# A fused decoder kernel: values of the sparse heads with the values stationary, and the weights divided by their sum on GpSimd

## The chip, the cores and the metric

The kernel runs on one core of a Trainium2 chip. The metric is the device time of one execution in microseconds (us). The core's engines each run a program of their own and wait for one another by semaphores: TensorE (PE, matmuls and transposes), VectorE (DVE), ScalarE (ACT), GpSimd (POOL), and the DMA queues. The kernel before takes 2286.29 us, the median of three runs (2286.06 to 2287.71).

## What is computed

A first block (attention, mLSTM, mixture of experts) feeds a second block of two equal layers over 512 tokens of width 1024. Each layer of the second has two kinds of attention, 8 sparse heads of 64 columns and 4 dense ones, then gates and an FFN. The change is in the sparse heads of the second block:

```
def sparse_attention(q, k, v, q_idx, k_idx, w_idx, k_sel):
    ...
        logits = jnp.einsum('bqhd,bqkhd->bqhk', qb, kg) * (dh ** -0.5)
        logits = jnp.where(valid[:, :, None, :], logits, -jnp.inf)
        p = jax.nn.softmax(logits, axis=-1).astype(v.dtype)
        return jnp.einsum('bqhk,bqkhd->bqhd', p, vg)
    ...
    ya = sparse_attention(aq, ak, av, iq, ik, iw, k_sel).reshape(B, S, D_A)
    ...
    g = jax.nn.sigmoid((gates + gate_bias))
    g_a, g_b = jnp.split(g, 2, axis=-1)
    merged = g_a * (ya @ w_up_a) + g_b * (yb @ w_up_b)
    x = x + merged @ w_out
```

The selection of the best 128 keys is done with a mask over all earlier keys, so the products run over whole rows of keys.

## The kernel before

**Units.** The attention stage of a layer (`pe_att2`) runs 48 units, one for each head of a block of 128 tokens: 0 to 15 are the dense heads (blocks 0 to 3), 16 to 47 the sparse heads, eight for each of blocks 4 to 7, which are the token rows i = 0 to 3 with 128(i+1) keys. A unit passes through the engines in steps. In step s TensorE makes the scores of units s and s+1 (sparse heads in pairs, on the row halves of the array, L1469), transposes the weights of unit s-3 (L1479, "turn") and multiplies those of unit s-4 with the values (L1487: one matmul for each 128 keys and head, stationary 128 turned weights, moving the 64 columns of the values). VectorE finds the least value of each row (L1493), ScalarE the exponential with its sum (L3426); the turned weights are copied out of PSUM by ScalarE for even units (L1504) and by VectorE for odd ones (L1502). After the last head of a sparse block VectorE takes the reciprocal of the eight sums (L3380) and multiplies the block's output by it (L3383); TensorE turns the block with four transposes (L1512, `pe_block_turned`); ScalarE and VectorE split it into a rounded high part and the rest (L1519, L1526).

**Dense work between.** Between these come parts of the big matmuls (`pe_between`), three to a step up to s = 31, then two, then one from s = 49. Each part is three kinds of matmuls (L686 to L688: high by high, low by high, high by low). The parts are counted by y. Parts 0 to 47 are the projections of the sparse heads; 48 to 111 use the gate's weight pieces 0 to 15, four parts to a piece; 112 to 119 are the places of the block turns, with no matmuls of weights; 120 to 135 use pieces 16 to 19, of the first up projection.

**Weight pieces.** Each piece comes by DMA, ScalarE makes its rounded high half (L637), GpSimd (in this stage) the low half, weights less high half (L674, `pool_lo`), and waits for nothing but the high half. The high halves have three buffers: that of piece p is made when the products of piece p-3 are done. Each engine's program is in fixed order. On GpSimd the stage is only the twenty low halves of a layer, in a row; ScalarE has its high halves between exponentials, copies and splits.

The profiled kernel's functions that the change touches:

## Time and profile before

| what | value |
|---|---|
| median of three runs | 2286.29 us |
| span of the profiled execution (its own time) | 2288.9 us |
| TensorE busy | 2188.9 us (96%) |
| VectorE, ScalarE, GpSimd busy | 54%, 37%, 16% |
| attention stage of the second block, first layer | about 842 to 1066 us |
| the same in the second layer | the same rows 788.4 us later |

A row of the timeline gives the start of a group of instructions, its length, and in brackets the idle time of the engine before it with what ended it. Consecutive instructions of a kind stand in one row with their count. Matmuls overlap in the rows: what one costs is the distance from its start to the next start. A row of a line's group gives how many, their busy time and the mean of one in ns. TensorE's granted clock is 1.00 at 2.4 GHz and 0.50 at 1.2 GHz.

### The profile page before, as it was taken

What the parts mean: (1) busy time and instruction counts of PE and PEld (TensorE: products, weight loads), DVE (VectorE), ACT (ScalarE), POOL (GpSimd) and SP (SyncE); (2) the same over time, 40 slices, a digit from 0 to 9 for tenths busy, and PEclk for the clock granted to TensorE, in tenths of its full rate; (3) what the DMA queues carried; (4) which work ended last, traced back from release to release, by engine and by line L of the source; (5) the groups of instructions that cost most, each with busy time, mean ns of one, the idle gap of its engine ahead of it and who ended that gap; (6) DMA issues with size and microseconds to landing.
All of it is one profiled execution on the core that took longest, in us unless ns stands there. A gap on an engine that the chain in (4) does not pass through costs nothing.

```text
span 2288.9 us, 28099 instructions
## 1 busy us (share of the span) xinstructions
PE 2188.9 (96%) x10757; PEld 1671.8 (73%) x10757; DVE 1238.6 (54%) x2370; ACT 847.1 (37%) x1493; POOL 358.4 (16%) x276
## 2 busy tenths in 40 slices
PE   7999998799998999999999999999999999999999
PEld 4786776543436767778788888877677787888887
DVE  4744557621326876675544334469667755453442
ACT  4444544311105455443432222344654433231231
POOL 0111124010002544320000000045433200000000
PEclk9999999889999999999999999999999999999999
DMA  8217301699992222212233232232222122323222
GB/s 303 66 47 230 129 29 48 251 385 409 409 407 87 74 74 56 82 57 65 84 110 101 94 99 92 81 91 83 66 64 82 51 81 92 102 92 101 92 86 80
DMA packets 175580, 288.01 MB, mean 126 GB/s; under 512 B 13486, under 2 KB 125656, under 8 KB 175448
## 3 DMA queue, kind: packets, MB, share of 16 engines
q1 hardware_dynamic: 173152, 278.73, 36.2%
q0 software_dynamic: 1152, 4.19, 0.5%
q10 hardware_dynamic: 1144, 3.29, 0.4%
q8 instruction: 87, 1.43, 0.2%
q14 instruction: 45, 0.37, 0.1%
HBM read 281.98 MB, written 4.19 MB: 125 GB/s over the span
## 4 chain that ended last, share of the span: by engine, by line
PE 80%; DVE 10%; DMA 3%; ACT 3%; issue 2%; SPq 1%; POOL 0%; DVEq 0%; ACTq 0%
PE PS L686 21%; PE PS L688 20%; PE PS L687 20%; PE PS L2496 4%; PE PS L1487 3%; PE PS L2537 2%; PE PS L1469 2%; PE PS L2557 1%; PE PS L1479 1%; SPq L3701 1%; DMA AR<-in_w_mod_dram 1%; DVE AL L868 1%; PE PS L1121 1%; PE PS L1667 1%; DVE CO L865 1%
## 5 line engine op out<-in xcount | busy, mean ns | idle before, releaser
L686 PE MATMUL PS<-OPH,WHI 128*128 128x512 f32 x1192 | 482.0, 404 | 5.5 <-DVE AR L1318 2.8
L688 PE MATMUL PS<-OPH,WLO 128*128 128x512 f32 x1192 | 467.7, 392 | 0.0
L687 PE MATMUL PS<-OPL,WHI 128*128 128x512 f32 x1192 | 466.5, 391 | 0.0
L637 ACT ACTIVATE WHI<-RAW 128x1024 fp32r<-128x1024 f32 (+2 forms) x282 | 292.9, 1041 | 457.4 <-PE PS L688 449.5
L658 DVE TENSOR_TENSOR WLO<-RAW,WHI 128x1024 fp32r<-128x1024 f32 (+1 forms) x187 | 224.3, 1202 | 368.7 <-ACT WHI L637 368.3
L674 POOL TENSOR_TENSOR WLO<-RAW,WHI 128x1024 fp32r<-128x1024 f32 (+1 forms) x95 | 229.8, 2422 | 928.9 <-ACT WHI L637 922.8
L686 PEld LDWEIGHTS PS<-OPH,WHI 128*128 128x128 f32 x1192 | 225.2, 189 | 61.0 <-issue 10.1
L688 PEld LDWEIGHTS PS<-OPH,WLO 128*128 128x128 f32 x1192 | 224.8, 189 | 48.5
L687 PEld LDWEIGHTS PS<-OPL,WHI 128*128 128x128 f32 x1192 | 225.5, 189 | 42.2 <-issue 1.0
L686 PE MATMUL PS<-WHI,OPH 128*128 128x512 f32 (+2 forms) x568 | 226.6, 399 | 9.0 <-DVE OPL L2196 2.5
L688 PE MATMUL PS<-WHI,OPL 128*128 128x512 f32 (+2 forms) x568 | 216.0, 380 | 0.0
L687 PE MATMUL PS<-WLO,OPH 128*128 128x512 f32 (+2 forms) x568 | 215.2, 379 | 0.0
L686 PEld LDWEIGHTS PS<-WHI,OPH 128*128 128x128 f32 x568 | 108.2, 190 | 46.4 <-issue 23.9
L686 PE MATMUL PS<-FR,WHI 128*128 128x512 f32 x352 | 136.9, 389 | 0.0
L687 PE MATMUL PS<-FR,WHI 128*128 128x512 f32 x352 | 136.9, 389 | 0.0
L688 PE MATMUL PS<-FR,WLO 128*128 128x512 f32 x352 | 136.9, 389 | 0.0
L688 PEld LDWEIGHTS PS<-WHI,OPL 128*128 128x128 f32 x568 | 108.1, 190 | 19.8
L687 PEld LDWEIGHTS PS<-WLO,OPH 128*128 128x128 f32 x568 | 108.3, 191 | 15.5 <-issue 0.5
L3426 ACT ACTIVATE AL<-AL,AC 128x128 f32<-128x128 f32 (+3 forms) x128 | 71.2, 557 | 106.2 <-DVE AC L1493 105.7
L686 PEld LDWEIGHTS PS<-FR,WHI 128*128 128x128 f32 x352 | 66.1, 188 | 13.8
L688 PEld LDWEIGHTS PS<-FR,WLO 128*128 128x128 f32 x352 | 66.1, 188 | 13.7
L687 PEld LDWEIGHTS PS<-FR,WHI 128*128 128x128 f32 x352 | 66.1, 188 | 13.6
(469 smaller groups left out, 3314.6 us busy)
## 6 DMA issues: line engine op xcount, KB each, us to landing
RAW<-in_w_in_dram SPq DMA_DIRECT2D x102, 512.0 KB, 3.7
RAW<-in_w_ffn_in_dram SPq DMA_DIRECT2D x88, 512.0 KB, 3.5
RAW<-in_w_ffn_out_dram SPq DMA_DIRECT2D x40, 512.0 KB, 3.4
RAW<-in_w_mod_dram SPq DMA_DIRECT2D x36, 512.0 KB, 4.7
ONCE<-in_w_down_dram SPq DMA_DIRECT2D x35, 512.0 KB, 15.8
RX<-in_w_gate_dram SPq DMA_DIRECT2D x29, 512.0 KB, 15.4
RAW<-in_w_out_dram SPq DMA_DIRECT2D x24, 512.0 KB, 3.4
RAW<-in_w_up_dram SPq DMA_DIRECT2D x20, 512.0 KB, 15.7
```

The source lines that it names most:

```text
L637: hi.up(A.e.activation(q.fhi, q.flat, ACT.Copy), ("w", q.i))
L658: lo_v.up(V.e.tensor_tensor(q.flo, q.flat, q.fhi.bitcast(F32), ALU.subtract), ("w", q.i))
L674: lo_p.up(G.e.tensor_tensor(q.flo, q.flat, q.fhi.bitcast(F32), ALU.subtract), ("w", q.i))
L686: T.e.matmul(o, a[0], b[0], start=first, stop=False)
L687: T.e.matmul(o, a[0], b[1], start=False, stop=False)
L688: return T.e.matmul(o, a[1], b[0], start=False, stop=last)
L865: t = row_v.up(V.e.tensor_reduce(c[:, 0:k], s3[:, n0:, :], X, ALU.add), (r, "sum"))
L1469: mm = T.e.matmul(PS[:, 512 * b + c0:512 * b + c0 + w], l_, r_, start=True, stop=True)
L1487: mm = T.e.matmul(u.o, u.pt[:, 128 * j:128 * j + 128], v_, start=(j == 0), stop=(j == nb - 1))
L2496: mm = T.e.matmul(PS[64 * i:64 * i + 64, 512 * b:512 * b + 512], XG[:, g % 3, 2 * n + k, 64 * i:64 * i + 64], q.raw[:, k, :], start=(n == ...
L2537: mm = T.e.matmul(PS[64 * i:64 * i + 64, o:o + 512], AE[:, g % 2, k, 64 * i:64 * i + 64], q.raw[:, 0, 512 * n:512 * n + 512], start=(k == ...
L3426: expd.up(A.e.activation(v.p, v.p, ACT.Exp, bias=v.nm, scale=-1.0, accum_out=v.rs), v.name)
```

## The change

The values of a sparse head become the stationary operand (64 columns) and the 128 turned weights move. Two heads of a pair use the two column halves of the array, so the output of a block comes out with the head's columns on partitions and tokens along the row: it is turned already. The values of both heads of a pair are issued together, at the odd head's step (`pe_pair_values`). The block turns of blocks 4 to 7 are gone, 16 transposes for each layer; the splits read PSUM itself (blocks 6 and 7) or a copy that VectorE makes of it (blocks 4 and 5). As a row's sum now lies along the moving side, the weights are divided ahead of their turn: VectorE takes the reciprocals of a pair's sums at each even step, and GpSimd multiplies each unit's weights by them (`evened`, new line L3007). TensorE's turn of a unit waits for that in place of the exponential. The low halves of the weight pieces are placed between the units on GpSimd by a rule of due parts. The copies of turned weights get four buffers in place of two. Line numbers grow by one up to the stage, by more in it (L674 is L675, L637 is L638, L1479 is L1480, L3426 is L3465).

```diff
pool_rope(rope_no[("aq", l), 0] + 4 * at[0] + at[1])
-            for pieces in J["gate", l] + J["upb", l]:
-                for i in pieces:
-                    pool_lo(i + 3)
+            units = units2(l)
+            later_ = [i + 3 for pieces in J["gate", l] + J["upb", l] for i in pieces]
+            y = 48
+            for s in range(16, len(units) + 2):
+                while later_ and y >= GATES0 + 4 * (20 - len(later_)) + 6:
+                    pool_lo(later_.pop(0))
+                if s >= 18:
+                    u = units[s - 2]
+                    G.wait_ge(*tidy["over", l, u.no])
+                    evened.up(G.e.tensor_scalar(u.p, u.p, u.over, None, ALU.mult), u.name)
+                y += parts_at(s)
+            for upto in later_:
+                pool_lo(upto)
...
                         pe_block_turned_b(l, i)
-                if y in (TURN0 + 5, TURN0 + 6):
-                    blk = y - TURN0 - 1
-                    pe_block_turned(("a2", l, blk), YR2[:, blk % 4], tidy["a2", l, blk], D)
...
                 if y in (TURN0 + 6, TURN0 + 7):
-                    blk = y - TURN0 - 2
-                    act_block_split(("a2", l, blk), OPH[:, 0:4, sparse_tokens(blk)])
+                    act_value_split(l, y - TURN0 - 2)
...
                 if y in (TURN0 + 6, TURN0 + 7):
-                    blk = y - TURN0 - 2
-                    c = sparse_tokens(blk)
-                    dve_block_split(("a2", l, blk), OPL[:, 0:4, c], OPH[:, 0:4, c])
+                    dve_value_split(l, y - TURN0 - 2)
...
         PTB2 = in_(AL, 23456, 1024).rearrange("p (i n) -> p i n", i=2)
-        YR2 = in_(AL, 14752, 2048).rearrange("p (i n) -> p i n", i=4)
+        PTC2 = in_(AL, 14752, 1024).rearrange("p (i n) -> p i n", i=2)
+        YT2 = in_(AL, 15776, 1024).rearrange("p (i g n) -> p i g n", i=2, g=4)
...
                     u.vs = [VAR[:, j, 64 * h:64 * h + 64] for j in range(i + 1)]
-                    u.o = ps(OUT2)[:, 64 * h:64 * h + 64]
+                    u.o = PS[hp:hp + 64, 512 * OUT2 + 128 * pr:512 * OUT2 + 128 * pr + 128]
+                    u.over = a8[:, 32 + h:33 + h]
...
-                u.pt = PTB2[:, u.no % 2, 0:u.n]
+                ring = PTB2 if u.kind == "b" or u.no % 4 < 2 else PTC2
+                u.pt = ring[:, u.no % 2, 0:u.n]
...
+        def turned_free(l, u):
+            if u.no in (18, 19):
+                return row_v[rope_no[("ak", l), 3], "done"]
+            return weighed["u", l, u.no - (2 if u.no < 18 else 4)]
...
-            return tidy["a2", l, blk], tidy["a2", l, blk]
+            done = tidy["a2", l, blk] if blk < 6 else split_v["a2", l, blk]
+            return done, done
+        def pe_pair_values(l, pair_):
+            for u in pair_:
+                T.wait_ge(*copied["pt", u.full])
+            n = len(pair_[0].vs)
+            for j in range(n):
+                for u in pair_:
+                    mm = T.e.matmul(u.o, u.vs[j], u.pt[:, 128 * j:128 * j + 128], start=(j == 0), stop=(j == n - 1))
+            weighed.up(mm, *[u.full for u in pair_])
+        def value_of(blk):
+            return YT2[:, blk - 4] if blk < 6 else ps(OUT2).rearrange("p (g n) -> p g n", g=4)
+        def act_value_split(l, blk):
+            if blk < 6:
+                A.wait_ge(*tidy["a2", l, blk])
+                A.wait_ge(*prod["gate", l, 7, 1])
+            else:
+                A.wait_ge(*weighed["u", l, 8 * blk - 9])
+            split_a.up(A.e.activation(OPH[:, 0:4, sparse_tokens(blk)], value_of(blk), ACT.Copy), ("a2", l, blk))
+        def dve_value_split(l, blk):
+            c = sparse_tokens(blk)
+            V.wait_ge(*split_a["a2", l, blk])
+            split_v.up(V.e.tensor_tensor(OPL[:, 0:4, c], value_of(blk), OPH[:, 0:4, c].bitcast(F32), ALU.subtract),
+                       ("a2", l, blk))
...
                     u = units[s - 3]
-                    T.wait_ge(*(diff_v["mix", l, u.no] if u.kind == "b" else expd[u.name]))
+                    T.wait_ge(*(diff_v["mix", l, u.no] if u.kind == "b" else evened[u.name]))
...
                         T.wait_ge(*copied[(u.kind + "v", l), t])
-                    pe_values(u, u.full)
-                    if u.blk == 7 and u.h == 3:
-                        pe_block_turned(("a2", l, 6), YR2[:, 2], tidy["a2", l, 6], D)
+                    if u.kind == "b":
+                        pe_values(u, u.full)
+                    elif u.h % 2:
+                        pe_pair_values(l, units[s - 5:s - 3])
                 some(dense, parts_at(s) - 2)
-            some(dense, 1)
-            pe_block_turned(("a2", l, 7), YR2[:, 3], tidy["a2", l, 7], D)
...
-            B.give(OUT2, (tidy, ("a2", l, 7)))
+            B.give(OUT2, (split_v, ("a2", l, 7)))
...
             for s in range(len(units) + 5):
+                if 18 <= s < len(units) + 2 and s % 2 == 0:
+                    u = units[s - 1]
+                    a8 = AC8[:, u.blk % 2, :]
+                    V.wait_ge(*expd[u.name])
+                    tidy.up(V.e.reciprocal(a8[:, 31 + u.h:33 + u.h], a8[:, 7 + u.h:9 + u.h]), ("over", l, u.no - 1), ("over", l, u.no))
...
                         if u.no >= 2:
-                            V.wait_ge(*weighed[units[u.no - 2].full])
+                            V.wait_ge(*turned_free(l, u))
...
                                   ("yb", l, u.blk))
-                    if u.last_head and u.kind == "a":
-                        a8 = AC8[:, u.blk % 2, :]
-                        V.wait_ge(*expd[u.name])
-                        t = tidy.up(V.e.reciprocal(a8[:, 32:40], a8[:, 8:16]))
-                        V.wait_ge(*t)
+                    if u.last_head and 4 <= u.blk < 6:
                         V.wait_ge(*weighed[u.full])
-                        tidy.up(V.e.tensor_tensor(YR2[:, u.blk % 4].rearrange("p (h e) -> p h e", h=8),
-                                                  ps(OUT2).rearrange("p (h e) -> p h e", h=8),
-                                                  a8[:, 32:40].unsqueeze(2).to_broadcast([128, 8, 64]), ALU.mult),
-                                ("a2", l, u.blk))
-                    if u.blk == 7 and u.h == 3:
-                        dve_block_split(("a2", l, 6), OPL[:, 0:4, sparse_tokens(6)], OPH[:, 0:4, sparse_tokens(6)])
+                        tidy.up(V.e.tensor_copy(YT2[:, u.blk - 4], ps(OUT2).rearrange("p (g n) -> p g n", g=4)), ("a2", l, u.blk))
+                    if u.last_head and u.blk >= 6:
+                        dve_value_split(l, u.blk)
...
                         if u.no >= 2:
-                            A.wait_ge(*weighed[units[u.no - 2].full])
+                            A.wait_ge(*turned_free(l, u))
...
-                    if u.blk == 7 and u.h == 3:
-                        act_block_split(("a2", l, 6), OPH[:, 0:4, sparse_tokens(6)])
+                    if u.last_head and u.blk >= 6:
+                        act_value_split(l, u.blk)
```

On GpSimd, before, the stage of a layer stands between the rotary steps of one stage and those of the next (WLO<-RAW,WHI are the low halves of weight pieces):

```order
L851 TENSOR_TENSOR AL<-AL 128x8x32 [waits row_v,row_a]
L851 TENSOR_TENSOR AL<-AL 128x8x32
L674 TENSOR_TENSOR WLO<-RAW,WHI 128x1024 [waits hi] x20
L674 TENSOR_TENSOR WLO<-RAW,WHI 128x648 [waits hi] x4
L851 TENSOR_TENSOR AL<-AL,RS 128x4x32 [waits row_v,row_a]
```

The twenty low halves follow one another with nothing between them. On GpSimd now, from the second unit of a pair (unit 37) to unit 45; AL<-AL,AC is a unit's weights times the reciprocals; the three low halves are those of pieces 17, 18 and 19:

```order
L3007 TENSOR_SCALAR AL<-AL,AC 128x384 [waits tidy]
L675 TENSOR_TENSOR WLO<-RAW,WHI 128x1024 [waits hi]
L3007 TENSOR_SCALAR AL<-AL,AC 128x384
L3007 TENSOR_SCALAR AL<-AL,AC 128x512 [waits tidy]
L675 TENSOR_TENSOR WLO<-RAW,WHI 128x1024 [waits hi]
L3007 TENSOR_SCALAR AL<-AL,AC 128x512
L3007 TENSOR_SCALAR AL<-AL,AC 128x512 [waits tidy]
L675 TENSOR_TENSOR WLO<-RAW,WHI 128x1024 [waits hi]
L3007 TENSOR_SCALAR AL<-AL,AC 128x512
L3007 TENSOR_SCALAR AL<-AL,AC 128x512 [waits tidy]
```

Behind low half 18 stand units 41 and 42, behind low half 19 units 43 to 47. On ScalarE, before, from the exponential of unit 43 over the copy of unit 40 and the splits of blocks 4 and 5 to the high halves of pieces 18 and 19 (WHI<-RAW):

```order
L3426 ACTIVATE AL,AC<-AL,AC 128x512 [waits least]
L1504 ACTIVATE AL<-PS 128x512 [waits turned,weighed]
L1519 ACTIVATE OPH<-PS 128x4x128 x2
L637 ACTIVATE WHI<-RAW 128x1024 [waits prod,raw2]
L3426 ACTIVATE AL,AC<-AL,AC 128x512 [waits least] x2
L1504 ACTIVATE AL<-PS 128x512 [waits turned,weighed]
L637 ACTIVATE WHI<-RAW 128x1024 [waits prod,raw3]
```

High half 18 follows two block splits. On ScalarE now, the same stretch:

```order
L3465 ACTIVATE AL,AC<-AL,AC 128x512 [waits least]
L1505 ACTIVATE AL<-PS 128x512 [waits turned,weighed]
L3315 ACTIVATE OPH<-PS 128x4x128 [waits weighed]
L3315 ACTIVATE OPH<-AL 128x4x128 [waits prod]
L3315 ACTIVATE OPH<-AL 128x4x128
L638 ACTIVATE WHI<-RAW 128x1024 [waits raw2]
L3465 ACTIVATE AL,AC<-AL,AC 128x512 [waits least] x2
L1505 ACTIVATE AL<-PS 128x512 [waits turned]
L638 ACTIVATE WHI<-RAW 128x1024 [waits prod,raw3]
```

The split of block 6 (from PSUM) stands ahead of the other two now, and high half 18 one split later. On TensorE, before, from the turn of unit 39 to the scores of units 44 and 45 (L1512 are turns of blocks 4 and 5, L1487 values of units 38 and 39):

```order
L1479 MATMUL PS<-cst,AL_64 128x128 [waits copy_a,expd]
L1479 MATMUL PS<-cst,AL_64 128x128 x2
L1512 MATMUL PS<-cst,AL_64 128x128 [waits split_v]
L1512 MATMUL PS<-cst,AL_64 128x128 x3
L1487 MATMUL PS<-AL_64 128x64 x3
L1512 MATMUL PS<-cst,AL_64 128x128 [waits split_v]
L1512 MATMUL PS<-cst,AL_64 128x128 x3
L1479 MATMUL PS<-cst,AL_64 128x128 [waits least,expd]
L1479 MATMUL PS<-cst,AL_64 128x128 x3
L1487 MATMUL PS<-AL_64 128x64 [waits copy_v]
L1487 MATMUL PS<-AL_64 128x64 x2
L1469 MATMUL PS<-AL_64 128x512 [waits least]
```

Two block turns lie between the turns of units 39 and 40. On TensorE now, the same stretch (L1480 turns, L3302 the pair's values):

```order
L1480 MATMUL PS<-cst,AL_64 128x128 [waits copy_a,evened]
L1480 MATMUL PS<-cst,AL_64 128x128 x2
L1480 MATMUL PS<-cst,AL_64 128x128 [waits least,evened]
L1480 MATMUL PS<-cst,AL_64 128x128 x3
L3302 MATMUL PS<-AL_64 64x128 [waits copy_v]
L3302 MATMUL PS<-AL_64 64x128 x5
L1470 MATMUL PS<-AL_64 128x512 [waits least]
L1470 MATMUL PS<-AL_64 128x512
```

The two block turns are gone, the values of unit 38 have moved behind the turn of unit 40 and joined those of 39, and each turn waits for GpSimd's `evened`.

## Rows read from the trace of the kernel before

**Rows 1.** The page: busy time, share of the span and instructions; shares of the chain.

```profile
PE 2188.9 (96%) x10757; PEld 1671.8 (73%) x10757; DVE 1238.6 (54%) x2370; ACT 847.1 (37%) x1493; POOL 358.4 (16%) x276
...
PE 80%; DVE 10%; DMA 3%; ACT 3%; issue 2%; SPq 1%; POOL 0%; DVEq 0%; ACTq 0%
```

**Rows 2.** Timeline of TensorE, first layer: start us, us, engine, line, operation, idle before.

```profile
1025.90 0.60 PE L1512 MATMUL PS<-cst,AL 128*128 128x128 f32 x4
1026.34 0.78 PE L1487 MATMUL PS<-AL 128*128 128x64 f32 x6
1026.95 0.61 PE L1512 MATMUL PS<-cst,AL 128*128 128x128 f32 x4
...
1031.10 0.60 PE L1479 MATMUL PS<-cst,AL 128*128 128x128 f32 x4
...
1032.93 1.00 PE L1487 MATMUL PS<-AL 128*128 128x64 f32 x8
1033.74 0.47 PE L686 MATMUL PS<-OPH,WHI 128*128 128x512 f32 x1
1034.06 0.39 PE L687 MATMUL PS<-OPL,WHI 128*128 128x512 f32 x1
```

**Rows 3.** Timeline of TensorE: column halves in the MoE; row halves (scores).

```profile
485.95 0.59 PE L2496 MATMUL PS<-FM 128*64 128x512 f32 x1
...
486.38 0.59 PE L2496 MATMUL PS<-FM 128*64 128x512 f32 x1
...
914.69 0.49 PE L1469 MATMUL PS<-AL 64*128 64x128 f32 x4
915.11 0.50 PE L686 MATMUL PS<-OPH,WHI 128*128 128x512 f32 x1
```

**Rows 4.** GpSimd by line and form, whole span: count, busy us, mean ns, idle before.

```profile
L674 POOL TENSOR_TENSOR WLO<-RAW,WHI 128x1024 fp32r<-128x1024 f32 x91 | 223.3, 2456 | 473.2 <-ACT WHI L637 467.1 <-DVE AL L899 6.1
...
L2057 POOL TENSOR_SCALAR AR<-AR,SM 128x128 f32<-128x128 f32 x40 | 24.5, 630 | 31.5 <-PE PS L1934 18.4 <-PE PS L1966 7.6 <-ACT SM L2002 5.5
...
L2060 POOL TENSOR_TENSOR AR<-AR 128x512 f32<-128x512 f32 x1 | 1.3, 1270 | 0.8 <-ACT AR L2024 0.8
...
L670 POOL CAST RH<-cst 128x1024 fp32r<-128x1024 f32 x1 | 1.0, 1042 | 4.4 <-PE PS L1953 4.4
```

**Rows 5.** Timeline of ScalarE, first layer, steps 41 to 46.

```profile
1025.00 0.72 ACT L3145 ACTIVATE AL<-AL,VT 128x512 f32<-128x512 f32 x1 [0.42 <-DVE AL L3196]
...
1028.65 1.08 ACT L1519 ACTIVATE OPH<-PS 128x512 fp32r<-128x512 f32 x2
1029.61 1.08 ACT L637 ACTIVATE WHI<-RAW 128x1024 fp32r<-128x1024 f32 x1
...
1037.30 1.06 ACT L637 ACTIVATE WHI<-RAW 128x1024 fp32r<-128x1024 f32 x1 [0.80 <-PE PS L688]
```

**Rows 6.** Timeline of GpSimd, first layer: low halves of pieces 18 and 19.

```profile
1030.77 2.40 POOL L674 TENSOR_TENSOR WLO<-RAW,WHI 128x1024 fp32r<-128x1024 f32 x1 [17.36 <-ACT WHI L637]
1038.44 2.40 POOL L674 TENSOR_TENSOR WLO<-RAW,WHI 128x1024 fp32r<-128x1024 f32 x1 [5.28 <-ACT WHI L637]
```

**Rows 7.** Timelines of VectorE and of TensorE, first layer, steps 20 and 21.

```profile
930.19 0.29 DVE L1493 CUSTOM_DVE_ANT_0 AL<-PS,AL 128x128 f32<-128x128 f32 x1
...
932.42 0.47 PE L686 MATMUL PS<-OPH,WHI 128*128 128x512 f32 x1
```

**Rows 8.** Timeline of TensorE, first layer: end of piece 16, turn of unit 43.

```profile
1036.81 0.40 PE L688 MATMUL PS<-OPH,WLO 128*128 128x512 f32 x1
...
1040.53 0.60 PE L1479 MATMUL PS<-cst,AL 128*128 128x128 f32 x4
```

**Rows 9.** Stretches: us, busy us of each engine (instructions), granted clock, DMA, GB/s.

```profile
105.70:108.10 2.40, 0.04 (x1) 0.00 (x0) 2.10 (x4) 2.40 (x6) 0.00 (x0) 1.00 0.00 0
108.40:111.80 3.40, 3.40 (x18) 3.40 (x18) 2.02 (x3) 0.44 (x1) 0.00 (x0) 0.50 0.05 8
1020.00:1030.00 10.00, 9.47 (x71) 7.56 (x72) 8.44 (x19) 8.66 (x19) 0.00 (x0) 1.00 0.00 1
```

More of the change, by code:

```diff
@@ L417, in body @@
     least, expd, sank, tidy = signal("least"), signal("expd"), signal("sank"), signal("tidy")
+    evened = signal("evened")
     gate_v, gate_a = signal("gate_v"), signal("gate_a")
@@ L3403, in dve_att2 @@
                 some(index_, best_at(s))
-            dve_block_split(("a2", l, 7), OPL[:, 0:4, sparse_tokens(7)], OPH[:, 0:4, sparse_tokens(7)])
             for _ in dense:
@@ L3449, in act_att2 @@
                 some(dense, parts_at(s))
-            act_block_split(("a2", l, 7), OPH[:, 0:4, sparse_tokens(7)])
             for _ in dense:
```

## The prediction

> **What bounds the kernel now.** I read the page's busy line and chain first: TensorE is busy for 96% of the span and 80% of the chain that ended last is TensorE [rows 1]. Work taken off TensorE is therefore gained wherever no other engine becomes late. The change touches only the attention stage of the second block, once per layer, and the rows of the second layer repeat those of the first 788.4 us later, so I work out one layer and double it. Inside the stage the timelines of TensorE, ScalarE and GpSimd have to be read side by side, since the change gives GpSimd work that TensorE waits for.
>
> **What TensorE is relieved of.** A sparse head's values in block 7 are eight matmuls, now from 1032.93 to 1033.74; the first dense matmul behind them takes 0.32 us to the next instead of 0.23 [rows 2], so a head holds TensorE for about 0.90 us, and a pair of heads 1.79. The eight start 0.11 us apart though only 64 columns move: they are bound by loading the stationary block. Six matmuls of block 6 cost 0.67 in the same way (1026.34 to 1026.95 is 0.61 [rows 2], and 0.06 to 0.09 behind), and by the same pitch the four of block 5 0.445, the two of block 4 0.22. The new form takes 8, 6, 4 or 2 passes per pair, each pass two matmuls on the two column halves. No row shows this form at 128 columns. Its nearest row is the MoE's: two column halves start together and the passes of 512 columns are 0.43 us apart [rows 3], so 128 columns stream in 0.107. I take 0.112 per pass, and 0.33 for going into and out of the halves, an estimate from the row halves of the scores, where two passes of 128 hold TensorE for 0.42 us (914.69 to 915.11 [rows 3]), 0.2 more than they stream, with 0.1 on the first dense matmul behind as there is today. A pair is then 0.55, 0.78, 1.00, 1.22 us in blocks 4 to 7, against 0.45, 0.89, 1.34, 1.79. Over four pairs each: +0.4, -0.5, -1.4, -2.3, together -3.7 us. The bounds of a pass are 0.055 (half of today's load) and 0.21 (the row halves' pass, where load and stream follow each other).
>
> The four block turns, four transposes each, took 0.44 us apiece (1025.90 to 1026.34 [rows 2]): -1.75. Four PSUM splits stay, from another source. So 5.45 us of TensorE work go per layer, 10.9 in both.
>
> **What GpSimd is given.** Before, it made only the low halves of the weight pieces here, 2.40 us each, and idled between. Now it also multiplies the weights of 32 units, in order with the low halves. No row has this instruction at 512 columns. At 128 it took 0.63; two-input work of 512 took 1.27, a one-input cast of 1024 took 1.04 [rows 4]. I take 1.1, between the last two, since one operand here is a scalar per row; bounds 0.8 and 2.5 (0.63 times four).
>
> By the Trainium skill (GPSIMD Engine Reference, Elementwise — side-by-side cycle accounting) a tight loop over 512 elements takes 769 ns, and its section Engine selection prefers VectorE for such work. By that figure each of the two terms below that hold one such instruction would be 0.33 us smaller, 1.3 us less in all. No run here shows it yet.
>
> **Where TensorE waits for it.** The order decides this. In the listing of the changed kernel GpSimd has low half 18 ahead of unit 41 and low half 19 ahead of unit 43. A low half waits for ScalarE's high half of the same piece. In the trace, ScalarE's row is unbroken from 1025.00 (but for issue): exponentials, splits, the copy of unit 40, two block splits, and only then high half 18 at 1029.61 [rows 5]. GpSimd had been idle for 17.4 us then and took low half 18 at 1030.77 [rows 6]. Nobody cared: piece 18 is used much later. Now unit 41 stands behind it.
>
> Shift up to there: values of blocks 4, 5 and half of 6 (+0.4 - 0.5 - 0.7), and one early wait. Unit 18 needs VectorE's reciprocal, which comes no earlier than 930.19; then 0.63 for the unit and 2.46 for low half 4, behind it, give 933.3, with the reciprocal itself some 0.1 more, against TensorE's use of piece 4 at 932.42 [rows 4, 7]: +1.0. Together +0.2. ScalarE has one more split ahead of high half 18 than before (block 6's), 0.54 us. So high half 18 ends at 1029.61 + 0.2 + 0.54 + 1.08 = 1031.4, low half 18 at 1033.9, unit 41 at 1035.0, TensorE's turn of unit 41 at 1035.1. It was at 1031.10 [rows 2]. **At this turn TensorE stands 4.0 us later than before**, whatever it gained ahead of it: the gains of steps 37 to 43 and two block turns are lost in that wait.
>
> Behind it stand four pairs of block 7 (-2.3) and two block turns (-0.9). Then the same again at unit 43: high half 19 waits for the last product of piece 16, whose last matmul starts at 1036.81; ScalarE starts 0.26 after its end (1037.30), 1.06, GpSimd 0.08 and 2.40, unit 43 1.1: 4.9 us after piece 16 [rows 5, 6]. TensorE needs 3.5 from there to the turn at 1040.53 [rows 8], 3.8 with a pair's values in place of a head's: **+1.0**. From unit 44 on GpSimd has only units, one to each step of TensorE, which is longer: nothing waits.
>
> **The clock.** TensorE's granted clock is 1.00 in this stage, between 1020 and 1030 as elsewhere, though no dense matmul runs there [rows 9]. But where it idled 2.4 us (105.70 to 108.10), the next 3.4 us ran at 0.50, 1.2 GHz [rows 9], and other idles of over 2 us in the trace are followed by the like. None of those under 2 us is. The idle ahead of turn 41 is the 4.0 and the gains spent in it, so well over 2. I take such a stretch as likely: half of 3.4, **+1.7**.
>
> **The sum.** Per layer +4.0 - 2.3 - 0.9 + 1.0 + 1.7 = +3.5; both layers +7.0. The profiled execution's span is 2288.9 us, which would become 2296; its runs' median is 2286.3, 2.6 below, so I predict 2286.3 + 7 = **2293 us**, 0.3% slower. What a measurement of this kernel can tell from no change is about 0.2%, 4.6 us. Its own range by the price of unit and pass is 2290 to 2296.
>
> **The rivals.**
> *No fall of the clock.* Same waits, +1.8 per layer: 2290. For it: one idle of over 2 us at the trace's start passed without a fall. Chance 0.21.
> *ScalarE is early enough (ends on the other side).* The place is high half 18. If it ended by 1027.5, low half 18 and unit 41 would be done when TensorE comes, and the 5.45 us less wait 1.0 and some 1.3 in the latency-bound steps 40 to 43 would remain: -3.1 per layer, 2280. It needs ScalarE's row to move up by 4 us; its links are the scores of unit 40 and its own exponentials, which do not get shorter. Against it: the unbroken row. Chance 0.17.
> *Cheap passes.* At 0.055 a pass the shift becomes about -1.8 and block 7's pairs give -4.1 instead of -2.3: some 4 us less per layer, 2285. Chance 0.09.
> *Dear passes.* If load and stream add up (0.107 + 0.055 = 0.16, up to 0.21), block 7 gives -0.6 or +0.8 and the shift ahead of turn 41 grows by 1.9 to 3.5: +3.5 to +6.5 more per layer, 2300 to 2306. Against it: the 128 by 64 loads of the MoE lie wholly beside the stream. Chance 0.10. By the Trainium skill (TensorEngine Tiling (Array Packing), Gotcha 2: Feature Incompatibilities) column tiling excludes the fast weight load, which would make this rival's load long; the MoE's passes at 0.43 for 512 columns show no such cost, though a load could hide there that 128 columns would not.
> *A dear unit.* At 2.4 us per 512 columns both waits grow by 1.3: 2298.5. Chance 0.09.
>
> **How the numbers follow.** Forecast 0.34, no fall 0.21, early ScalarE 0.17, dear passes 0.10, cheap passes 0.09, dear unit 0.09. Slower by over 0.2% (above 2290.9): 0.27 of the forecast, 0.04 of no fall, both dear cases: 0.50. Faster (below 2281.7): early ScalarE, and 0.03 of cheap passes: 0.20. The rest, 0.30, is within. The range 2280 to 2300 leaves out the dear passes and the lower half of early ScalarE, under 2 in 10.
>
> **What would show it.** Right: an idle of TensorE of several microseconds ahead of unit 41's turn (a few before 1035 in the first layer), released by GpSimd's new line, with ScalarE's high half 18 at its root; a smaller one at unit 43; GpSimd's row without gaps from high half 18 to unit 42; granted clock near 0.5 behind turn 41; eight passes of a pair in some 1.2 us. Wrong: turn 41 without an idle, low half 18 starting before 1029, or a pair of block 7 at 1.6 us and more.

## The result, and the profile after

The changed kernel takes 2299.72 us (median of four runs, 2298.13 to 2301.18), the kernel before beside it 2287.0: a ratio of 1.0046, 95% interval 1.0032 to 1.006. Run again beside another set it was 1.0056 (1.0041 to 1.007). Of 2286.3 us that is 7.3 to 16 us; 7 had been forecast. The change makes the kernel slower.

The page of the changed kernel, to be read beside [rows 1] (busy time, share of the span, instructions of each engine):

```profile
PE 2181.3 (95%) x10725; PEld 1649.0 (72%) x10725; DVE 1234.2 (54%) x2390; ACT 846.9 (37%) x1493; POOL 426.8 (19%) x340
```

TensorE is busy for 7.6 us less and GpSimd for 68 us more. So work did leave TensorE; what came is waiting. Whole spans compare badly here, since the first block, which nothing touches, came out between 5.4 us shorter and 1.5 longer from one execution to another, the after shown here 4.0 shorter. The stage itself is compared between the same two matmuls instead: the first with gate piece 0, and one at the stage's end. The timeline of TensorE before, first and second layer (start us, length, engine, line, operation):

```profile
903.54 0.47 PE L686 MATMUL PS<-OPH,WHI 128*128 128x512 f32 x1 [1.31 <-ACT WHI L637]
...
1064.82 0.39 PE L686 MATMUL PS<-OPH,WHI 128*128 128x512 f32 x1
...
1691.94 0.47 PE L686 MATMUL PS<-OPH,WHI 128*128 128x512 f32 x1 [1.31 <-ACT WHI L637]
...
1853.22 0.39 PE L686 MATMUL PS<-OPH,WHI 128*128 128x512 f32 x1
```

The same four matmuls of the changed kernel:

```profile
899.52 0.47 PE L687 MATMUL PS<-OPH,WHI 128*128 128x512 f32 x1 [1.30 <-ACT WHI L638]
...
1066.14 0.39 PE L687 MATMUL PS<-OPH,WHI 128*128 128x512 f32 x1
...
1693.17 0.47 PE L687 MATMUL PS<-OPH,WHI 128*128 128x512 f32 x1 [1.30 <-ACT WHI L638]
...
1860.55 0.39 PE L687 MATMUL PS<-OPH,WHI 128*128 128x512 f32 x1
```

The stage took 161.28 us in both layers; now 166.62 and 167.38: +5.3 and +6.1, together 11.4. In this execution TensorE's work between the layers and behind them moved by under 0.1 us; only the last transfers, of the output, end 0.4 us later. The table gives this difference, to within 0.01 us, for every kernel that follows.

| kernel | layer 1, us | layer 2, us | ratio to the kernel before (95%) |
|---|---|---|---|
| changed | +5.34 | +6.11 | 1.0046 (1.0032 to 1.006) |
| changed, again | +5.34 | +6.24 | 1.0056 (1.0041 to 1.007) |
| weights not divided | -5.46 | -5.40 | 0.9959 (0.9945 to 0.9972) |
| low halves 18, 19 moved | -2.74 | -2.74 | 0.9977 (0.9968 to 0.9986) |
| high half 18 early | -0.94 | -0.95 | 0.9994 (0.9985 to 1.0004) |
| units 41, 43 twice | +11.08 | +10.55 | 1.0106 (1.009 to 1.0121) |
| idle filled | +3.86 | +3.86 | 1.0032 (1.0021 to 1.0043) |
| own reciprocals, low half 4 first | -4.24 | -4.24 | 0.9967 (0.9954 to 0.998) |
| and low halves 16, 17 later | -4.90 | -4.84 | 0.996 (0.9945 to 0.9975) |
| on VectorE, one input | -1.16 | -1.14 | 0.9986 (0.9977 to 0.9995) |
| on VectorE, two inputs | +0.53 | +2.17 | 1.0018 (1.0009 to 1.0027) |

**What TensorE waits for** in the first layer's stage (engine and line, what released it, total us, times, longest):

```profile
PE PS L1480 <- POOL AL L3007: 7.5, 5, 4.5
PE PS L687 <- ACT WHI L638: 1.3, 1, 1.3
PE PS L687 <- issue: 1.1, 1, 1.1
```

The first row is new: five turns wait for GpSimd's multiplication. The second stood before too. Two smaller waits are for VectorE, 0.5 us (there before) and 0.4 us (new). "issue" at L687 is the first use of piece 4, at 929.49; low half 4 had ended on GpSimd just then, at 929.39. The two longest in TensorE's timeline, which answer to [rows 2] and [rows 8]:

```profile
1027.48 0.40 PE L689 MATMUL PS<-OPH,WLO 128*128 128x512 f32 x1
1032.34 1.12 PE L1480 MATMUL PS<-cst,AL 128*128 128x128 f32 x4 [4.47 <-POOL AL L3007]
1033.11 0.78 PE L687 MATMUL PS<-OPH,WHI 128*128 128x512 f32 x1
1033.68 0.63 PE L688 MATMUL PS<-OPL,WHI 128*128 128x512 f32 x1
...
1044.33 0.66 PE L1480 MATMUL PS<-cst,AL 128*128 128x128 f32 x4 [1.54 <-POOL AL L3007]
```

These are the turns of units 41 and 43. Behind the first the matmuls start 0.43 us apart (1033.68, 1034.11, ...) instead of 0.23. GpSimd at the same time, to be read beside [rows 6]:

```profile
1022.14 1.56 POOL L3007 TENSOR_SCALAR AL<-AL,AC 128x512 f32<-128x512 f32 x1 [0.63 <-DVE AC L3385]
1028.39 2.35 POOL L675 TENSOR_TENSOR WLO<-RAW,WHI 128x1024 fp32r<-128x1024 f32 x1 [4.68 <-ACT WHI L638]
1030.72 3.10 POOL L3007 TENSOR_SCALAR AL<-AL,AC 128x512 f32<-128x512 f32 x2
1040.35 2.38 POOL L675 TENSOR_TENSOR WLO<-RAW,WHI 128x1024 fp32r<-128x1024 f32 x1 [6.53 <-ACT WHI L638]
1042.71 7.74 POOL L3007 TENSOR_SCALAR AL<-AL,AC 128x512 f32<-128x512 f32 x5
```

GpSimd finished unit 40 at 1023.7, then idled 4.68 us for high half 18, although unit 41's reciprocal had been there since 1022.04. Low half 18, unit 41, and TensorE goes on at once. ScalarE's row, beside [rows 5]:

```profile
1025.72 0.60 ACT L3315 ACTIVATE OPH<-PS 128x512 fp32r<-128x512 f32 x1
1026.20 1.16 ACT L3315 ACTIVATE OPH<-AL 128x512 fp32r<-128x512 f32 x2
1027.24 1.07 ACT L638 ACTIVATE WHI<-RAW 128x1024 fp32r<-128x1024 f32 x1
...
1039.21 1.06 ACT L638 ACTIVATE WHI<-RAW 128x1024 fp32r<-128x1024 f32 x1 [0.85 <-PE PS L689]
```

Three block splits, then high half 18: the order that the listing had shown. Last the granted clock (stretch, its length, busy us of PE, PEld, DVE, ACT, POOL with counts, then the clock), behind turn 41 in the first layer, behind turn 43 in the first, and behind turn 41 in the second:

```profile
1033.10:1036.50 3.40, 3.40 (x12) 2.75 (x11) 1.23 (x2) 0.00 (x0) 0.73 (x1) 0.62 0.17 57
1044.30:1047.70 3.40, 3.37 (x18) 2.83 (x19) 2.05 (x4) 0.00 (x0) 3.40 (x3) 1.00 0.41 137
1826.00:1829.40 3.40, 3.40 (x11) 2.82 (x12) 0.69 (x1) 0.00 (x0) 1.39 (x1) 0.50 0.36 125
```

Ahead of turn 41 TensorE had idled 4.47 us in both layers, ahead of turn 43 1.54. In the second layer the low clock (1.2 GHz) lasts longer, which is most of the 0.8 us by which that layer is worse.

### The profile page after: what moved, and what is told of

The parts are those of the page before. It is cut to its first block, busy times and chain, and to the rows that moved or that the text cites. A ratio compares the mean times of both kernels' runs of the same rounds, so it can differ in the third digit from the quotient of the medians.

```text
span 2296.6 us, 28115 instructions
## 1 busy us (share of the span) xinstructions
PE 2181.3 (95%) x10725; PEld 1649.0 (72%) x10725; DVE 1234.2 (54%) x2390; ACT 846.9 (37%) x1493; POOL 426.8 (19%) x340
## 4 chain that ended last, share of the span: by engine, by line
PE 77%; DVE 11%; DMA 4%; ACT 4%; issue 2%; POOL 1%; SPq 1%; DVEq 0%; ACTq 0%
PE PS L687 21%; PE PS L689 20%; PE PS L688 20%; PE PS L2497 3%; PE PS L2538 2%; PE PS L1488 2%; PE PS L1470 1%; PE PS L2558 1%; PE PS L1480 1%; SPq L3739 1%; ACT WHI L638 1%; DMA AR<-in_w_mod_dram 1%; DVE AL L869 1%; DVE CO L866 1%; DMA ONCE<-in_w_down_dram 1%
## 5 line engine op out<-in xcount | busy, mean ns | idle before, releaser
L687 PE MATMUL PS<-OPH,WHI 128*128 128x512 f32 x1192 | 480.0, 403 | 7.7 <-DVE AR L1319 2.8
L638 ACT ACTIVATE WHI<-RAW 128x1024 fp32r<-128x1024 f32 (+2 forms) x282 | 293.1, 1041 | 465.0 <-PE PS L689 456.9
L675 POOL TENSOR_TENSOR WLO<-RAW,WHI 128x1024 fp32r<-128x1024 f32 (+1 forms) x95 | 229.6, 2420 | 759.4 <-ACT WHI L638 753.4
L687 PEld LDWEIGHTS PS<-OPH,WHI 128*128 128x128 f32 x1192 | 225.1, 189 | 67.5 <-issue 17.5
L687 PE MATMUL PS<-WHI,OPH 128*128 128x512 f32 (+2 forms) x568 | 226.9, 400 | 9.0 <-DVE OPL L2197 2.5
L687 PEld LDWEIGHTS PS<-WHI,OPH 128*128 128x128 f32 x568 | 108.2, 190 | 46.4 <-issue 24.0
L687 PE MATMUL PS<-FR,WHI 128*128 128x512 f32 x352 | 136.9, 389 | 0.0
L3465 ACT ACTIVATE AL<-AL,AC 128x128 f32<-128x128 f32 (+3 forms) x128 | 71.0, 556 | 111.7 <-DVE AC L1494 111.3
L3007 POOL TENSOR_SCALAR AL<-AL,AC 128x128 f32<-128x128 f32 (+3 forms) x64 | 70.1, 1104 | 119.9 <-DVE AC L3385 119.9
L687 PEld LDWEIGHTS PS<-FR,WHI 128*128 128x128 f32 x352 | 66.1, 188 | 13.7
```

The costliest lines, as they stand in the source:

```text
L638: hi.up(A.e.activation(q.fhi, q.flat, ACT.Copy), ("w", q.i))
L675: lo_p.up(G.e.tensor_tensor(q.flo, q.flat, q.fhi.bitcast(F32), ALU.subtract), ("w", q.i))
L687: T.e.matmul(o, a[0], b[0], start=first, stop=False)
L3007: evened.up(G.e.tensor_scalar(u.p, u.p, u.over, None, ALU.mult), u.name)
L3465: expd.up(A.e.activation(v.p, v.p, ACT.Exp, bias=v.nm, scale=-1.0, accum_out=v.rs), v.name)
```

## Experiments

**The theory** is the prediction's: TensorE's gain is real, and GpSimd's order gives more than all of it back. The rivals: the new form of the values brings nothing; GpSimd is too slow wherever the work stands; the low clock has another cause.

### The values alone

This kernel leaves out the division by the sum: GpSimd has low halves alone, and a turn waits for the exponential again.

```diff
-                if s >= 18:
-                    u = units[s - 2]
-                    G.wait_ge(*tidy["over", l, u.no])
-                    evened.up(G.e.tensor_scalar(u.p, u.p, u.over, None, ALU.mult), u.name)
...
-                    T.wait_ge(*(diff_v["mix", l, u.no] if u.kind == "b" else evened[u.name]))
+                    T.wait_ge(*(diff_v["mix", l, u.no] if u.kind == "b" else expd[u.name]))
```

> The weights are not divided by their sum at all (GpSimd's multiplications are left out, the turns wait for the exponential again); the values in column halves, the splits and the missing block turns stay, so this shows TensorE's side alone. Theory: 5.45 us of TensorE work less per layer, of which some 1.3 is eaten in the steps without dense work: -4 per layer, 2279 us, and no idle of TensorE at a turn. Rival (the new form of the values is itself no gain): 2284 or more.

Measured: ratio 0.9959, -5.46 and -5.40 us in the stage. So the expected -4 per layer was too cautious: the stage loses all of the 5.45 us worked out from the rows, although TensorE has three new waits for VectorE there, 0.8 us together. (The time, 2279.7, is near the expected 2279, but the kernel before took 2288.3 beside it.) A pair of block 7, with the dense matmuls around it (timeline of the changed kernel):

```profile
1049.17 0.40 PE L689 MATMUL PS<-OPH,WLO 128*128 128x512 f32 x1
1049.50 1.09 PE L3302 MATMUL PS<-AL 128*64 128x128 f32 x16
1050.53 0.50 PE L687 MATMUL PS<-OPH,WHI 128*128 128x512 f32 x1
1050.87 0.40 PE L688 MATMUL PS<-OPL,WHI 128*128 128x512 f32 x1
```

0.33 us into it instead of 0.23, 1.03 for it, 0.34 out of it instead of 0.23: 1.24 us, against 1.22 forecast and 1.79 before. Cheap and dear passes both fall.

### GpSimd's order

Low half 18 behind unit 43, low half 19 behind unit 45:

```diff
-                while later_ and y >= GATES0 + 4 * (20 - len(later_)) + 6:
+                while later_ and (y >= GATES0 + 4 * (20 - len(later_)) + 6 if len(later_) > 4 else s >= 54 - 2 * len(later_)):
```

> The changed kernel, with low half 18 on GpSimd moved behind unit 43 and low half 19 behind unit 45; nothing else differs. Theory (the order on GpSimd: unit 41 stands behind a low half that waits for ScalarE): TensorE's idles of 4.5 us at the turn of unit 41 and 1.5 at unit 43 are gone in both layers, with them the stretch at half clock; TensorE comes to turn 41 some 0.6 us later than before by its own work, then gains 3.2, so about -2.5 us per layer against the kernel before, 2282 us. Rival (GpSimd is too slow for both kinds of work wherever they stand): waits of like size come back at units 42 to 47 or at the first use of pieces 18 and 19, 2292 or more.

Measured: ratio 0.9977, -2.74 us in both layers, 8 to 9 us per layer better than the changed kernel. TensorE's waits for GpSimd in this stage:

```profile
PE PS L1480 <- POOL AL L3007: 1.4, 3, 0.7
```

Of 7.5 us 1.4 are left, at units 34, 36 and 40, and no wait came at the pieces 18 and 19. The same work on the same engine, two instructions moved in a row: GpSimd was not too slow.

### ScalarE's order

The other end of the same wait. GpSimd's order stays; ScalarE makes high half 18 at step 40:

```diff
+            elif y == TURN0:
+                act_hi(J["upb", l][0][0] + 3)
```

> The changed kernel with GpSimd's order as it is, but ScalarE makes high half 18 four steps earlier (at step 40, where it idles 3.6 us). Theory: the root of the idle at unit 41 is ScalarE's row, so low half 18 runs behind unit 40 at about 1023.7 to 1026 and the idle at 41 falls from 4.5 us to under 0.5, the half clock with it; the idle at 43 stays near 1.5, since high half 19 waits for piece 16. About -1 us per layer against the kernel before, 2285 us. Rival (GpSimd's own pace): the low half and the unit, 3.9 us together, still leave an idle of 2 us or more at unit 41, 2294.

Measured: ratio 0.9994 (no difference from before), -0.94 us in the stage, as expected. The idle at unit 41 is gone: its turn starts 0.23 us behind the matmul ahead of it, at 1031.09. That at unit 43 is 1.54 as it was. GpSimd here:

```profile
1025.53 1.56 POOL L3007 TENSOR_SCALAR AL<-AL,AC 128x512 f32<-128x512 f32 x1 [0.67 <-DVE AC L3387]
1027.06 2.38 POOL L675 TENSOR_TENSOR WLO<-RAW,WHI 128x1024 fp32r<-128x1024 f32 x1
1029.40 1.57 POOL L3007 TENSOR_SCALAR AL<-AL,AC 128x512 f32<-128x512 f32 x1
```

Low half 18 runs in the gap between units 40 and 41. So the root of the idle at 41 was ScalarE's row, through GpSimd's.

### The price of a unit on that path

```diff
+                    if u.no in (41, 43):
+                        G.wait_ge(*evened.up(G.e.tensor_scalar(u.p, u.p, u.over, None, ALU.mult)))
```

> The changed kernel with units 41 and 43 multiplied a second time on GpSimd (one more instruction of 1.55 us each, ahead of the one that TensorE waits for). Theory: GpSimd's row from high half 18 to turn 41 and from high half 19 to turn 43 is the path, so the idles become 6.0 and 3.1 us, +3.1 per layer at least, 2304 to 2307 us. Rival (TensorE is held there by something else, GpSimd only finishes about then): the time stays within 1 us of the changed kernel's 2298 to 2301.

Measured: ratio 1.0106, +11.08 and +10.55 us in the stage, 5.7 and 4.4 more than the changed kernel. The two turns in TensorE's timeline:

```profile
1039.44 1.11 PE L1480 MATMUL PS<-cst,AL 128*128 128x128 f32 x4 [6.12 <-POOL AL L3009]
...
1054.06 0.66 PE L1480 MATMUL PS<-cst,AL 128*128 128x128 f32 x4 [3.20 <-POOL AL L3009]
```

The idles grew by 1.65 and 1.66, as expected: this row is the path. But the time grew by more than these 3.3 us. The clock in the stretches behind both turns:

```profile
1039.40:1042.80 3.40, 3.36 (x10) 2.88 (x11) 0.69 (x1) 0.00 (x0) 1.53 (x1) 0.50 0.02 5
1054.00:1057.40 3.40, 3.34 (x12) 2.78 (x13) 1.78 (x3) 0.00 (x0) 3.08 (x3) 0.66 0.00 0
```

Behind the idle of 1.54 us at unit 43 the clock had stayed at 1.00 in the changed kernel; behind 3.20 it fell. That had not been in the expectation.

### The clock by itself

Forty transposes of a constant, in the place of the idle ahead of turn 41:

```diff
+            for _ in range(filler):
+                T.e.transpose(ps(b)[:, 0:128], ident, ident)
+            if filler:
+                T.wait_ge(*evened[u.name])
...
-                    T.wait_ge(*(diff_v["mix", l, u.no] if u.kind == "b" else evened[u.name]))
-                    pe_weights_turned(u, u.full)
+                    if u.no != 41:
+                        T.wait_ge(*(diff_v["mix", l, u.no] if u.kind == "b" else evened[u.name]))
+                    pe_weights_turned(u, u.full, 40 if u.no == 41 else 0)
```

> The changed kernel with 40 transposes of a constant, 4.4 us of TensorE, in the place where it idles ahead of the turn of unit 41; their result is overwritten by the turn. Theory (the idle itself lowers the granted clock behind it): GpSimd finishes at the same time as before, so the turn comes when it did, but the stretch behind it runs at 1.00 instead of 0.5 to 0.6, and each layer gains 1.1 to 1.7 us: 2 to 3.5 us less than the changed kernel's 2298 to 2301. Rival (the low clock there has another cause, or costs nothing): no difference.

Measured: ratio 1.0032, +3.86 us in both layers: 1.48 and 2.25 less than the changed kernel. The forty transposes, then the turn:

```profile
1031.26 4.53 PE L1480 MATMUL PS<-cst 128*128 128x128 f32 x40
1035.93 0.66 PE L1484 MATMUL PS<-cst,AL 128*128 128x128 f32 x4
```

The turn comes 132.85 us behind the stage's first matmul, against 132.82. The clock behind it, where it was 0.62 and 0.50:

```profile
1036.30:1039.70 3.40, 3.40 (x20) 2.83 (x19) 1.46 (x3) 0.00 (x0) 1.12 (x1) 1.00 0.30 105
1829.10:1832.50 3.40, 3.40 (x20) 2.85 (x19) 1.46 (x3) 0.00 (x0) 1.12 (x1) 1.00 0.31 106
```

The turn came when it did, and only the clock behind it differs. So it was the idle that lowered the clock, and the price is 1.48 and 2.25 us, where the prediction had 1.7.

### The waits that are left

Low half 4 ahead of unit 18, and a reciprocal for each unit in place of one for a pair:

```diff
-                while later_ and (y >= GATES0 + 4 * (20 - len(later_)) + 6 if len(later_) > 4 else s >= 54 - 2 * len(later_)):
+                while later_ and (y >= GATES0 + 4 * (20 - len(later_)) + (2 if len(later_) == 18 else 6) if len(later_) > 4 else s >= 54 - 2 * len(later_)):
...
-                if 18 <= s < len(units) + 2 and s % 2 == 0:
+                if 17 <= s < len(units) + 1:
...
-                    tidy.up(V.e.reciprocal(a8[:, 31 + u.h:33 + u.h], a8[:, 7 + u.h:9 + u.h]), ("over", l, u.no - 1), ("over", l, u.no))
+                    tidy.up(V.e.reciprocal(a8[:, 32 + u.h:33 + u.h], a8[:, 8 + u.h:9 + u.h]), ("over", l, u.no))
```

> As the run with low halves 18 and 19 moved, and two more: low half 4 ahead of unit 18, and a reciprocal for each unit instead of each pair, those of even units one step earlier. Theory: the idle of 1.1 us at the first use of piece 4 goes, and those at the turns of units 34, 36 and 40 (0.4, 0.35, 0.7), which wait for a pair's reciprocal, go or fall below 0.2. That is 2 to 2.5 us per layer less than that run, close to the 5.45 of TensorE's work: 2278 us. Rival (other waits take their place, in steps 40 to 43 above all): under 1 us per layer, 2281 or more.

Measured: ratio 0.9967, -4.24 us in both layers, 1.5 better than with the order alone: less than the 2 to 2.5 expected, more than the rival's 1. The idle at piece 4 went, and that at unit 34; the one at 40 stayed at 0.7, and at 36 another, of 0.8, took the old one's place, released by VectorE. Its last instructions of the selection in this kernel, L2831 being the last of the mask:

```profile
1013.13 0.69 DVE L2828 MAX8 AL<-AL 128x8 f32<-128x512 f32 x1
...
1013.93 0.68 DVE L2829 MATCH_REPLACE8 AL<-AL 128x512 f32<-128x512 f32 x1
1014.64 1.07 DVE L2831 TENSOR_SCALAR AL<-AL 128x512 f32<-128x512 f32 x1
```

and GpSimd beside them:

```profile
1013.02 2.42 POOL L675 TENSOR_TENSOR WLO<-RAW,WHI 128x1024 fp32r<-128x1024 f32 x1
```

In the kernel before L2831 takes 0.43 us; here it ends 0.27 behind the low half. The two instructions ahead of it, which read and write SBUF as well, keep their 0.69 and 0.68. Low halves 16 and 17 were then moved behind units 38 and 39:

```diff
-                while later_ and (y >= GATES0 + 4 * (20 - len(later_)) + (2 if len(later_) == 18 else 6) if len(later_) > 4 else s >= 54 - 2 * len(later_)):
+                while later_ and (y >= GATES0 + 4 * (20 - len(later_)) + (2 if len(later_) == 18 else 6) if len(later_) > 6 else s >= {6: 41, 5: 42, 4: 46, 3: 48}.get(len(later_), 99)):
```

> As the run with each unit's own reciprocal, and low halves 16 and 17 on GpSimd moved behind units 38 and 39 (they are used 8 us or more later). In that run TensorE still idled 0.8 us at the turn of unit 36, released by VectorE; there VectorE's last instruction of the selection mask took 1.07 us beside low half 16, against 0.43 in the kernel before. Theory (GpSimd's low half held it): the mask instruction takes 0.43 us again, the idle at unit 36 falls below 0.3, and each layer is 0.5 to 0.8 us shorter: 2280 to 2281 us. Rival (VectorE is late there for its own queue): the mask instruction is as short, but the idle stays at 0.7 or more and the time does not move.

```profile
1013.77 0.43 DVE L2831 TENSOR_SCALAR AL<-AL 128x512 f32<-128x512 f32 x1
```

Measured: ratio 0.996 (0.9945 to 0.9975), -4.90 and -4.84 us, the idle at unit 36 is 0.2. So the low half had held the mask instruction, and this VectorE's row. By the stage this is the fastest of the complete kernels, 0.4% faster than the kernel before; of TensorE's 5.45 us only 0.6 are lost.

### The multiplications on VectorE

GpSimd keeps to low halves; VectorE multiplies both units of a pair behind their reciprocals:

```diff
-                if s >= 18:
-                    u = units[s - 2]
-                    G.wait_ge(*tidy["over", l, u.no])
-                    evened.up(G.e.tensor_scalar(u.p, u.p, u.over, None, ALU.mult), u.name)
...
+                    V.wait_ge(*t)
+                    for u in units[s - 2:s]:
+                        evened.up(V.e.tensor_scalar(u.p, u.p, u.over, None, ALU.mult), u.name)
```

> The multiplications on VectorE, both units of a pair behind their reciprocal, and GpSimd as in the kernel before with low halves alone. Theory: no idle at units 41 and 43 and none at piece 4; VectorE takes some 10 to 15 us of work per layer, up to 0.7 per unit, hidden but for steps 40 to 43, where it is 84% busy and TensorE has no dense matmuls: up to 2.8 us per layer there. 2280 to 2284 us. Rival (VectorE becomes late for the masks and least values all along): 2288 or more.

Measured: ratio 0.9986, -1.15 us in the stage, slower than expected, with idles of 1.20 and 1.72 us at the turns of units 36 and 42, both released by VectorE. VectorE around the second of them, and later:

```profile
1031.08 3.10 DVE L3384 TENSOR_SCALAR AL<-AL,AC 128x512 f32<-128x512 f32 x2
...
1036.70 0.88 DVE L3384 TENSOR_SCALAR AL<-AL,AC 128x512 f32<-128x512 f32 x2
```

GpSimd beside the first:

```profile
1031.11 2.38 POOL L675 TENSOR_TENSOR WLO<-RAW,WHI 128x1024 fp32r<-128x1024 f32 x1 [19.16 <-ACT WHI L638]
```

Two units take 0.88 us alone and 3.10 where low half 18 runs; of these the first takes 2.70 and ends 0.29 behind the low half. The two-input form was the test of whether the fast form is what is held:

```diff
-                        evened.up(V.e.tensor_scalar(u.p, u.p, u.over, None, ALU.mult), u.name)
+                        evened.up(V.e.tensor_tensor(u.p, u.p, u.over.to_broadcast([128, u.n]), ALU.mult), u.name)
```

> As the run with the multiplications on VectorE, but in the form with two inputs, the second being the reciprocal read again for every column, in place of the form with one input and a scalar. In that run the 512-column form took 0.48 us alone and 2.70 us where it started beside a low half of GpSimd (2.38 us), and ended just behind it. Theory (the fast one-input form needs what GpSimd's instruction holds, and waits for its end): the two-input form takes about 0.69 us with or without a low half beside it, TensorE's idles of 1.7 and 1.2 us go below 0.7, and the time falls by 1 to 2 us per layer, to 2282 to 2284 us. Rival (any VectorE instruction that reads only SBUF is held there): it takes 2.5 us or more beside a low half too, and the time is 2286 or more.

Measured: ratio 1.0018, +0.53 and +2.17 us. VectorE beside low half 18 (both instructions, then the second of them by itself), and alone:

```profile
1035.04 3.48 DVE L3384 TENSOR_TENSOR AL<-AL,AC 128x512 f32<-128x512 f32 x2
1035.64 2.87 DVE L3384 TENSOR_TENSOR AL<-AL,AC 128x512 f32<-128x512 f32 x1
...
1047.62 1.29 DVE L3384 TENSOR_TENSOR AL<-AL,AC 128x512 f32<-128x512 f32 x2
```

and GpSimd's low half beside the first:

```profile
1035.07 2.89 POOL L675 TENSOR_TENSOR WLO<-RAW,WHI 128x1024 fp32r<-128x1024 f32 x1 [19.83 <-ACT WHI L638]
```

The two-input form waits as well, so the theory of the fast form fell. The first of the two ran on, and the low half begun beside it took 2.89 instead of 2.38; the second took 2.87 and ended 0.55 behind the low half. The rival came true in its numbers, but as it was put, for any VectorE instruction that reads only SBUF, it is too wide: the two selection instructions above were not held.

The two layers differ by 1.64 us here. TensorE idled 2.09 us ahead of unit 42 in the first, 2.07 in the second; behind the first the granted clock stayed at 1.00 (1039.30 to 1042.70), behind the second it was 0.65 (1828.80 to 1832.20).

### The changed kernel again

No edit.

> The changed kernel itself once more, on the chip of the run beside it, for the size of the change. Stage by stage its execution should show +5.3 to +6.1 us per layer against the kernel before, of which the time shows 10 to 12 us: 2297 to 2299 where the kernel before takes 2287.

Measured: ratio 1.0056, 2301.78 beside 2290.35; the stages +5.34 and +6.24, with the same idles at units 41 and 43 to 0.01 us.

## Why the prediction was right, and where its sizes were off

Direction, place and mechanism came as forecast: TensorE idles ahead of unit 41, GpSimd at its head, ScalarE's high half 18 at the root, a smaller idle at unit 43, a low clock behind the first. The sum was +3.5 us per layer, the measured one +5.3 and +6.1. That the time lies inside the stated 2280 to 2300 is in part luck: 2299.72 is inside by 0.3 us and above the 2290 to 2296 that the prices of unit and pass were to span, and the changed kernel run again took 2301.78. Step by step:

- **TensorE's work**, -5.45: measured -5.46 and -5.40 with the weights undivided.
- **A unit of 512 columns on GpSimd**, 1.1 taken between 1.04 and 1.27 of [rows 4]: 1.565 (mean of sixteen). It lies above the two-input row, so that row was no upper neighbour. The row of 128 columns, 0.63, was the right start; the new rows run 0.67, 0.93, 1.25, 1.565, some 0.30 for each 128 columns more. So 1.1 was too low, though inside its bounds of 0.8 and 2.5; that puts 0.46 us into each of the two waits. The Trainium skill's 769 ns for 512 elements in a tight loop (GPSIMD Engine Reference, Elementwise — side-by-side cycle accounting) is half of what the trace shows; the measurement decides.
- **Turn 41**, +4.0: measured from the stage's first matmul, 132.82 us against 127.56, +5.26. Of the missing 1.26 the unit has 0.46. The rest is the shift ahead of it, taken as +0.2: the scores of unit 40 came 1.0 late. The wait at piece 4 was forecast at 1.0 and cost 1.1 and TensorE's restart; what the prediction did not see are 0.4 us each at units 34 and 36, which wait for a pair's reciprocal on VectorE. I had put the reciprocals down as short, and not asked when VectorE reaches them.
- **Behind it**: four pairs and two block turns, -3.2, by the pair's row above 1.24 instead of 1.22. Turn 43, +1.0: an idle of 1.54, mostly the unit's 0.46 again.
- **The clock**, +1.7: 1.48 and 2.25 by the filled idle. The reading under it was wrong in one point: that none of the idles under 2 us in the trace of before is followed by a fall. Behind one of 1.54 us (up to 328.62), and behind one of 1.36 us (up to 698.70, close behind another of 1.10), the clock was low:

```profile
328.62:331.50 2.88, 2.88 (x7) 2.30 (x8) 2.00 (x10) 1.22 (x10) 1.70 (x3) 0.50 0.04 9
698.70:702.00 3.30, 3.30 (x13) 3.30 (x14) 1.78 (x3) 1.25 (x2) 0.00 (x0) 0.54 0.00 0
```

Behind 1.54 us at turn 43 of the changed kernel it stayed at 1.00. The length of the last idle alone does not tell.

So the mis-sized terms are the unit's price and the shift. Idles also cost a little more than their number: it is counted from a matmul's modelled end, 0.40 us behind its start in the row at 1027.48, where the next would have started after 0.23, so 0.17 for each. Of the rivals, an early ScalarE was right as a mechanism when it was made so, but not as a price: 2280 was put on it, and the early high half alone gives -0.94 per layer, because high half 19 waits for piece 16 whatever ScalarE does. The dear unit was true for a third of the way (1.565 between 1.1 and 2.4). The clock did fall, and passes were neither cheap nor dear. The Trainium skill's advice to swap the operands and tile columns where the moving side has 64 columns or fewer (TensorEngine Tiling (Array Packing), When to Use Tiling) agrees with the trace: 1.24 us for 1.79.

## What to carry to other kernels

When work is added to an idle engine, read its program in order, and ask of each instruction ahead of the new one what that waits for: GpSimd had time for all units, and 8 us in each layer hung on two instructions that could have stood three units later. A new wait of several microseconds on TensorE can cost more than its length: behind idles of 3.20 and 4.47 us here the clock fell, and the longer one cost 1.5 to 2.3 us beyond itself. Where an operation has a row at one size only, take that row and the row in proportion as the bounds for another size (0.63 and 2.5 here; it was 1.57), rather than a cheaper operation's row as a neighbour. And ask for the small instructions ahead of it when they are reached, not only how long they are.

## What the runs showed of the hardware

VectorE and GpSimd's low halves exclude each other for some forms of VectorE's instructions. On VectorE a multiplication of 128x512 from SBUF to SBUF takes 0.48 us alone (0.69 in the two-input form); started beside a low half on GpSimd of 2.38 us it takes 2.70 (2.87), and a mask instruction of 0.43 took 1.07. Instructions that read PSUM beside a low half kept their 0.68 (the least values at 1028.24 and 1028.83 in the changed kernel, with low half 18 from 1028.39 on), and so did two instructions of the selection from SBUF to SBUF, MAX8 (0.69) and MATCH_REPLACE8 (0.68), beside low half 16. The Trainium skill says that the two share their SBUF interfaces, with contention where VectorE uses both ports or has two SBUF inputs (GPSIMD Engine Reference, Specifications). The runs fit this, though no view shows the ports.
